# The experts' token rows and gated products stored in the order in which the transposes read them

## What is computed

```python
x = _layernorm(DEEPNORM_ALPHA * x + g_a * y_lat, ln1_g[l], ln1_b[l])
u = x * (1.0 + sc_f) + sh_f              # the rows that the experts read
# each token goes to 8 of 64 experts
hdn = silu(xr @ w_gate[e]) * (xr @ w_up[e])   # xr: rows of u, 1024 wide; hdn: 256 wide
y = hdn @ w_down[e]                            # 256 -> 1024
out[token] += weight * y
```

## Time and profile before

| What | Value |
|---|---|
| median of 3 runs | 3100.55 us |
| lowest and highest run | 3096.86 and 3107.66 us |
| profiled execution, its own time | 3100.06 us |
| its span (first to last instruction) | 3097.6 us |
| mean granted clock of TensorE | 0.931 |
| busy: PE, weight loads, DVE, ACT, POOL | 87%, 52%, 40%, 22%, 18% |
| moved by DMA | 659.14 MB |

### The profile page before, as it was taken

How to read it: one execution, slowest core, us unless ns; L and a number is a source line. 1 busy time by engine, 2 the same in 40 slices (tenths; PEclk the granted TensorE clock), 3 DMA queues, 4 the chain that set the end, 5 groups by cost and what they waited for, 6 DMA issues and landing times. The chain is left out here.

```text
span 3097.6 us, 60060 instructions
## 1 busy us (share of the span) xinstructions
PE 2694.1 (87%) x23131; PEld 1617.4 (52%) x23131; DVE 1251.2 (40%) x3448; ACT 691.6 (22%) x1594; POOL 562.1 (18%) x556
## 2 busy tenths in 40 slices
PE   7988987699988899999999589898699598888885
PEld 4566456444446455555555245546586455444442
DVE  1045467400045455555555433467502433323334
ACT  1245444200001111111111214544200111111111
POOL 0010034100000232332233001024201022222220
PEclk9999988799998899999999889998799699999997
DMA  7188110112220999999997722010143589999995
GB/s 253 45 264 298 57 56 4 57 60 76 81 72 27 372 372 361 367 360 357 372 347 287 290 71 82 2 55 4 39 147 106 215 352 405 400 399 403 402 400 195
DMA packets 205963, 659.14 MB, mean 213 GB/s; under 512 B 28294, under 2 KB 40376, under 8 KB 188272
## 3 DMA queue, kind: packets, MB, share of 16 engines
q1 hardware_dynamic: 171132, 590.67, 49.8%
q0 software_dynamic: 28000, 50.64, 4.4%
q10 hardware_dynamic: 6676, 15.58, 1.4%
HBM read 648.07 MB, written 49.89 MB: 225 GB/s over the span
## 5 line engine op out<-in xcount | busy, mean ns | idle before, releaser
L2332 PE MATMUL PS<-BIG 128*64 128x256 f32 x5440 | 656.0, 396 | 70.7 <-issue 67.4
L2332 PEld LDWEIGHTS PS<-BIG 128*64 128x64 f32 x5440 | 408.9, 143 | 270.7 <-issue 102.4
L2252 POOL DMA_INDIRECT BIG<-u_d,IXG x176 | 180.5, 1026 | 880.6 <-DVE IXG L2396 862.3
L2304 PE MATMUL PS<-BIG 128*64 128x512 f32 x1360 | 329.3, 605 | 5.2 <-ACT BIG L2366 5.2
L1818 PE MATMUL PS<-UT,BIG 128*128 128x512 f32 (+1 forms) x768 | 254.8, 493 | 7.4 <-PEq L2676 4.2
L2359 ACT ACTIVATE BIG<-PS 64x256 f32<-64x256 f32 x170 | 64.0, 376 | 762.2 <-PE PS L2332 762.2
L1818 PEld LDWEIGHTS PS<-UT,BIG 128*128 128x128 f32 x768 | 147.3, 193 | 114.4 <-issue 104.0
L2257 POOL DMA_INDIRECT y_d<-BIG,IXS x174 | 177.5, 1020 | 80.9 <-issue 54.9
L2423 DVE TENSOR_TENSOR BIG<-BIG,PS 64x256 f32<-64x256 f32 x170 | 72.2, 425 | 259.4 <-ACT BIG L2359 259.3
L1898 DVE TENSOR_TENSOR BIG<-BIG,PS 128x512 f32<-128x512 f32 (+1 forms) x48 | 26.6, 554 | 365.9 <-PE PS L1831 365.9
L1119 PE MATMUL PS<-UT,BIG 128*128 128x512 f32 x384 | 173.0, 605 | 0.0
(11 more groups left out here) (391 smaller groups left out, 3459.7 us busy)
## 6 DMA issues: line engine op xcount, KB each, us to landing
BIG<-in_w_exp_gate SPq DMA_DIRECT2D x136, 1024.0 KB, 9.7
BIG<-in_w_exp_up SPq DMA_DIRECT2D x136, 1024.0 KB, 12.2
BIG<-in_w_exp_down SPq DMA_DIRECT2D x136, 1024.0 KB, 16.4
BIG<-in_w_ada SPq DMA_DIRECT2D x24, 2048.0 KB, 8.6
BIG<-in_w_in SPq DMA_DIRECT2D x22, 2048.0 KB, 8.4
BIG<-y_d SPq DMA_DIRECT2D x24, 1024.0 KB, 16.4
BIG<-in_w_out SPq DMA_DIRECT2D x4, 2048.0 KB, 8.0
BIG<-mod_d ACTq DMA_DIRECT2D x12, 512.0 KB, 6.0
```

Of the source, the lines that this page charges most:

```text
L2252: e.indirect_dma_start(out=XG[:, q, :], out_offset=None, in_=u_d.rearrange("t (h n) -> (t h) n", h=2), in_offset=bass.IndirectOffsetOnAxis ...
L2304: mm = e.matmul(PS[half(c), 5 + q, :], HT[:, q, k, :], W[:, sl, w:w + 512], start=k == 0, stop=k == 1)
L2332: mm = e.matmul(PS[half(c), 2 + q, 0:FE], xt, W[:, sl, w:w + FE], start=k + hf == 0, stop=k + hf == 4)
```

## The change

Three places change. In `stage_merge` ACT no longer writes `u` itself. It copies it into a new buffer `up` with the columns of each half reordered, so that the 128 columns of each transpose lie together, and writes `up`. DVE, which reuses `u` for a later tile, now waits for that copy and not for the write. In the experts L2288 reads 128 adjacent columns of `XG`. DVE's product reads both its inputs with a step of two elements and writes `HB` with each parity's 128 columns together, and L2342 reads 128 adjacent columns of `HB`. Sizes, transfers, weights and the number of matmuls stay.

```diff
+            up = ar(B0 + 1024, 2, D)
...
                     e.wait_ge(s_u, i + 1)
-                    e.dma_start(u_d[t * P:(t + 1) * P, :], u[:, i % 2, :]).then_inc(s_ud[i % 2], 16)
+                    if i >= 2:
+                        e.wait_ge(s_ud[i % 2], 16 * (i // 2))
+                    e.activation(up[:, i % 2, :].rearrange("p (h k q) -> p h k q", h=2, k=4), u[:, i % 2, :].rearrange("p (h q k) -> p h k q", h=2, k=4), ACT.Copy).then_inc(s_up, 1)
+                    e.wait_ge(s_up, i + 1)
+                    e.dma_start(u_d[t * P:(t + 1) * P, :], up[:, i % 2, :]).then_inc(s_ud[i % 2], 16)
...
                         e.wait_ge(s_tp, 2 * (ti - 1))
-                        e.wait_ge(s_ud[ti % 2], 16 * (ti // 2))
+                        e.wait_ge(s_up, ti - 1)
...
                 for k in range(4):
-                    mm = e.transpose(PS[:, q, k * P:(k + 1) * P], XG[:, q, k::4], ident)
+                    mm = e.transpose(PS[:, q, k * P:(k + 1) * P], XG[:, q, k * P:(k + 1) * P], ident)
...
                         for k in range(2):
-                            mm = e.transpose(PS[:, 4, k * CAP:(k + 1) * CAP], HB[:, q, k::2], ident[half(1), half(1)])
+                            mm = e.transpose(PS[:, 4, k * CAP:(k + 1) * CAP], HB[:, q, k * P:(k + 1) * P], ident[half(1), half(1)])
...
-                        e.tensor_tensor(HB[:, q, :], SGL[:, q, :], PS[half(1), 2 + q, 0:FE], ALU.mult).then_inc(s("h", q), 1)
+                        pairs_of = lambda v: v.rearrange("p (c k) -> p k c", k=2)
+                        e.tensor_tensor(HB[:, q, :].rearrange("p (k c) -> p k c", k=2), pairs_of(SGL[:, q, :]), pairs_of(PS[half(1), 2 + q, 0:FE]), ALU.mult).then_inc(s("h", q), 1)
```

More of the change, by code:

```diff
@@ L1791, in stage_merge @@
             nm = f"s_mg_"
-            s_gp, s_sg, s_op, s_tm, s_mt, s_ld, s_yp, s_ye, s_var, s_std, s_nx, s_next, s_t1, s_u, s_tp, s_te = (
-                sem(nm + x) for x in ("gp", "sg", "op", "tm", "mt", "ld", "yp", "ye", "var", "std", "nx", "next", "t1", "u", "tp", "te"))
+            s_gp, s_sg, s_op, s_tm, s_mt, s_ld, s_yp, s_ye, s_var, s_std, s_nx, s_next, s_t1, s_u, s_tp, s_te, s_up = (
+                sem(nm + x) for x in ("gp", "sg", "op", "tm", "mt", "ld", "yp", "ye", "var", "std", "nx", "next", "t1", "u", "tp", "te", "up"))
             s_ud = [sem(f"{nm}ud{i}") for i in range(2)]
```

## The result

The changed kernel takes 3081.05 us, the median of seven runs (3073.44 to 3084.82). Seven runs of the kernel before, between them, give 3100.55 us (3092.17 to 3107.66). The ratio is 0.9933, with a 95% interval of 0.9917 to 0.9949. The profiled execution has a span of 3079.1 us, against 3097.6 before.

What follows compares the result with a forecast made beforehand. PE was taken to bound layer 0's experts, weight transfers layer 1's. 3100.06 - 19.8 (layer 0's transposes) + 0.3 (copy delaying the writes) - 0.4 (layer 1) = 3080.2 us, forecast as 3081; range 3075 to 3092.

Steps and rivals of the forecast that it cites:

- The low bound of 0.065 us: Product transposes in the experts: least saving per pair, if only the first load gets shorter; 0.115 us was taken.
- What lies on the path: Layer 0 experts: both savings count in blocks two to six, only the product transposes' in the first; 19.8 us.
- Weights: Layer 0 experts: faster turns raise 362 GB/s to 373, weights still arrive in time; costed at nothing.
- The product: DVE's product in the experts: reading both inputs with a step of two costs nothing, 0.41 to 0.43 us.
- Rival (b): The product pays for its step in a turn's first block, 3.1 us; time about 3084; chance 0.12.
- The copy: ACT's copy in the merge: 1.06 us for 1024 elements per partition, 0.7 us more if its step costs.
- the dear end: ACT's copy in the merge, if its step costs as much per element as DVE's step of 64: 0.7 us more.
- What it costs in time: Last merge write of each layer, issued later by the copy: +0.15 us taken; bounds -0.9 and +1.1, dear copy +1.8.
- The prediction's own sign: Merge: the last write lands within 1 us of its old distance from the last operation of u.
- Layer 1: Layer 1 experts: transfers set the time; only one block's savings at either end, 0.4 us in all.
- (a): The product transposes get no faster; 8.1 us from the gathered rows' transposes alone, 3092; chance 0.12.
- (c): The product becomes the bound: 1.2 us growth takes the whole gain, 2.0 us gives near 3148; chance 0.04.

Runs made afterwards that it cites:

- e1: Changed kernel with the product and its transposes left as before, so only the copy and the adjacent reads of gathered rows; 3096.47 us, ratio 0.998 to the kernel before.
- e2: Changed kernel without the copy and with the gathered rows read at the old step, so only the product and its transposes change; 3089.47 us, ratio 0.9953.
- e8: Changed kernel without ACT's copy; DVE writes u in the new order, reading with steps of four, router and shared expert weights loaded to fit; 3090.18 us, one run.
- e5: Changed kernel with the merge copy keeping the column order and the gathered rows read with a step of four; 3086.39 us, one run.
- e6: Changed kernel with the merge copy reading adjacent elements and writing with a step of 128; 3091.0 us, one run, the kernel before 3109.27 in that job.
- e3: Changed kernel with the gathered rows' transposes reading at a step of two, experts' columns in a wrong order; 3098.04 us, one run.
- e7: Changed kernel with DVE doing the product twice in each block; 3113.69 us, one run.
- e11: Changed kernel without the copy, DVE writing u in the new order, beside the unedited changed kernel (3094.3 us); 3089.52 us, ratio 0.9928 to the kernel before.

## Why the prediction came out right

The forecast was 3081 us, and it took 3081.05. That close an agreement is luck: the seven runs lie between 3073.44 and 3084.82, and the 2.4 us of scatter in the combine stage are more than all the small terms of the sum. The sum behind it is right in its large term and wrong in one small one that was hidden.

- **L2294: right.** 0.09 us per block was forecast at 0.095, loads 140 ns, and e1 alone gives 8.2 us for 8.1.
- **L2348: right.** The pair takes 0.33 us, as worked out from a row with twice the streamed columns. The low bound of 0.065 us is excluded by e2 (every block of a turn 0.11 to 0.12 us shorter, 12.6 us in the stage).
- **What lies on the path: right.** Middle blocks 6.44 us as forecast; in the first block only L2348 counts (5.22 to 5.10), and e1, with the shorter L2294 alone, leaves it at 5.22. The sum was 19.8 us and the stage shows 19.7, but part of that is chance. From the first gate/up matmul to the stage's end it is 18.5 us less, and 1.2 us fell away before it, where PE waited for the first gathered rows. The 17 first blocks give only 0.6 us (90.9 to 90.3) of the 2.0 counted, because the first two of them took 7.85 and 5.99 us, against 7.49 and 5.22 before.
- **Weights: right.** At 372 GB/s (373 forecast) no wait for a weight transfer stands among those of PE in layer 0 (one weight load waited for one, 1.2 us, ahead of the stage's first block, where PE also stood for 0.9 us until ACT's copy was done).
- **The product: right.** Among the groups by shape it is:

```profile
L2430 DVE TENSOR_TENSOR BIG<-BIG,PS 64x256 f32<-64x256 f32 x170 | 72.1, 424 | 258.5 <-ACT BIG L2365 258.4
```

  424 ns with a step of two on both inputs, 0.42 before. Rival (b) falls. The Trainium skill's rule of pairs of adjacent words (Vector Engine (DVE) Microarchitecture Reference, Measured stream behaviour on trn2) does not hold for this instruction, which reads one input from PSUM. It does fit e8, where `u` reads two inputs in SBUF with a step of four: 1.96 us / 1024 = 1.9 ns per element against 1.22 / 1024 = 1.2, within the 1.75 to 2.5 that the page gives for small steps.
- **The copy: the term that was mis-sized.** Forecast were 1.06 us, 1.8 at the dear end; it takes 2.04 to 2.08. The dear end took DVE's price of a step for ACT's. The step costs ACT 1.0 us for 1024 elements, about 1 ns each, on either side of the copy (e5, e6).
- **What it costs in time: right by its cover in layer 0, too low in layer 1.** +0.15 us per layer were forecast; the router began 0.05 us later in layer 0 and 1.24 us later in layer 1, where the route stage is 0.5 us longer. In layer 0 the write met the shared expert's weights when it was issued at once (4.6 us) and ran nearly by itself when issued 2.1 us later (2.6): the last of these weights landed 3.35 us after the write's issue before, 1.03 after. So the delay was paid back in full. That was the prediction's lower bound, 2.0 us off the transfer, and e5 shows the same with a delay of 1.1 us. In layer 1 the landing took 4.1 us before and 3.3 after, so there only 0.8 of 2.1 us came back. In e1 and e3 it took 4.8 us with the same copy, the router began 7.01 us after `u`, and the route stage took 43.3 us instead of 40.2, so the copy can cost 3 us there; that is beyond the prediction's bound of 1.8. The prediction's own sign, a landing within 1 us of its old distance from `u`, holds in layer 0 and not in layer 1 (1.2 us later). (Its range, too, counted 1.1 us a layer at the high end and not the 1.8 of its dear copy, with which it would end at 3092.) The landing of the last write in layer 1, in e1:

```profile
u_d<-BIG ACTq DMA_DIRECT2D x1, 512.0 KB, 4.8
```

  A packet of instruction code passes the DMA engines beside this write in layer 1 and not in layer 0, in the changed kernel, e1 and e3 from about 2.7 to 3.7 us after the issue. The write's last packet ends at 3.7 us in e1 and e3, and at 2.75 in the changed kernel. Whether the code packet is what holds it was not tried.
- **Layer 1: right in that nothing is gained there.** 584.5 against 585.4 us, and 582.9 to 585.1 in the other kernels, with loads long or short. There the transfers set the time. The 0.4 us of the sum is smaller than this scatter, so no run shows it.
- **The rivals.** (a) falls with the loads at 138 ns. Its two readings, the shape and the line of 16 bytes (the Trainium skill, SBUF — State Buffer, Door 1: The DMA port swizzle), both fall with e3: 209 ns at full shape with a step of two, where two reads fall on one such line. (c) did not happen, but e7 speaks for a break-even that was set too high. The 1.2 us of growth that should have taken the gain counted the wait alone; 0.42 us of growth cost 16.3 us net in e7's one trace, with 10.1 us of slow second blocks behind the longer waits. Where the first block is short the wait would be about 1.0 us after the same growth (an estimate, 0.52 + 0.45); waits of 1.0 to 1.1 us cost no second block its clock in e6 and e8 to e11.

## What to carry to other kernels

A transpose on PE is a weight load, so look at the load's own row: a load of columns that lie apart took half as long again here, with a step of two as with one of four, and putting the order into an operation that exists already can be free (the product, 424 ns either way) or cheaper than a copy of its own (the sum, 0.7 us against 2.04). Before costing a delay of a transfer, look at what the transfer meets when it goes out; a write that waits for the traffic to end can land at the same time. An edit that lays data out anew can also change how large the packets of a transfer are, which then has to be told apart from the rest of the edit. And a wait that PE pays once a turn can grow until the clock falls behind it: its price is then more than its length.

## What had not been expected of the hardware

- A weight load of 128 columns with a step of two takes 209 ns, with a step of four 213, with none 140.
- ACT's copy of 1024 elements takes 1058 ns plain, 2076 with a step of four on the read and 2008 with a step of 128 on the write.
- A write of 512 KB took 4.6 us at one moment and 2.6 two microseconds later.
- In the two jobs of e6 to e11, on two chips, ACT's first SiLU of a turn begins 6.2 to 6.4 us after its loop's branch, in the other runs 5.73; the first block of a turn is then 0.5 to 0.6 us longer. What ACT does in that time stays open.
- After 1.5 to 1.7 us of idle PE the granted clock fell in six of seventeen cases (e7 and e2); after 1.4 us or less it never did at this place. After the same 2.04 us ahead of layer 0's last shared expert it was 0.72 in e8 and 1.00 in the changed kernel.
